# VectorE order around the gates: convolution channel 7 placed ahead of them, and the second layer's second S5 half placed behind the convolution

## The reference, cut to what matters

```python
for l in range(DEPTH):
    h = x @ w_in[l]
    s5_u, mq, mk, mv, gq, gk, gv, gz, ga, gb = _split(h, IN_SIZES)
    y_s5 = s5_mixer(s5_u, ...)          # states = associative_scan(a1*a2, a2*s1+s2)
    y_moba = moba_mixer(mq, mk, mv)
    y_gdn = gdn_mixer(gq, gk, gv, gz, ga, gb, ...)
    x = layer_norm(DEEPNORM_ALPHA * x + concat([y_s5, y_moba, y_gdn]) @ w_out[l], ...)
    f = swiglu(x, ...) if l % 2 == 0 else moe_ffn(x, ...)
    x = layer_norm(DEEPNORM_ALPHA * x + f, ...)

def gdn_mixer(q, k, v, z, a, b, conv_w, a_log, dt_bias, norm_w):
    qkv = silu(causal_conv(concat([q, k, v]), conv_w))      # 4 taps for each of 3*384 channels
    qh, kh = l2norm(heads(q)) * HEAD_DIM ** -0.5, l2norm(heads(k))
    beta = sigmoid(b)
    g = -exp(a_log) * softplus(a + dt_bias)                 # the gates
    o = chunk_gated_delta(qh, kh, heads(v), g, beta)        # solves (I + L) U = rhs in chunks of 64
```

## Time and profile before

| | us |
|---|---|
| time of the kernel before, median of 3 runs | 1582.57 (1580.28 to 1582.84) |
| the profiled execution, its own time | 1582.77 |
| span of the trace in it | 1581.0 |
| PE busy / DVE busy / ACT busy / POOL busy | 1538.6 / 1258.3 / 957.8 / 100.2 |

### The profile page before, as it was taken

How to read it: one execution, slowest core, us unless ns; L and a number is a source line. 1 busy time by engine, 2 the same in 40 slices (tenths; PEclk the granted TensorE clock), 3 DMA queues, 4 the chain that set the end, 5 groups by cost and what they waited for, 6 DMA issues and landing times.

```text
span 1581.0 us, 24154 instructions
## 1 busy us (share of the span) xinstructions
PE 1538.6 (97%) x9412; PEld 1268.5 (80%) x9412; DVE 1258.3 (80%) x1224; ACT 957.8 (61%) x811; POOL 100.2 (6%) x134
## 2 busy tenths in 40 slices
PE   8998999999998899999999999999999999999996
PEld 6777688888897767888888888888888888888875
DVE  6856854444788786888888888888888888888897
ACT  1175144334436524777777777777777777777774
POOL 0012180000000401000000000000000000000201
PEclk9999999999999999999999999999999999999999
DMA  9412488885354035999999999999999999999994
GB/s 335 161 55 82 160 318 307 279 280 186 107 175 173 9 131 200 395 393 394 395 396 361 395 396 350 395 396 349 395 396 351 395 396 349 395 396 368 398 394 162
DMA packets 195769, 473.12 MB, mean 299 GB/s; under 512 B 7712, under 2 KB 22176, under 8 KB 194640
## 3 DMA queue, kind: packets, MB, share of 16 engines
q1 hardware_dynamic: 191552, 454.23, 77.5%
q0 software_dynamic: 4144, 17.88, 2.9%
HBM read 464.21 MB, written 25.69 MB: 310 GB/s over the span
## 4 chain that ended last, share of the span: by engine, by line
PE 88%; DVE 7%; DMA 2%; issue 1%; ACT 1%; SPq 0%; DVEq 0%; ACTq 0%; POOLq 0%
PE ps L1865 47%; PE ps L1876 23%; PE ps L1815 4%; PE ps L1938 2%; PE ps L1843 1%; PE ps L2337 1%; PE ps L2333 1%; DVE arena L1197 1%; PE ps L1827 1%; DMA arena<-in_md 1%; DVE unit_lo L1295 1%; DMA arena<-in_w_in 1%; PE ps L2096 1%; PE ps L2233 0%; PE ps L2143 0%
## 5 line engine op out<-in xcount | busy, mean ns | idle before, releaser
L1289 DVE TENSOR_TENSOR lo<-arena,hi 128x2048 fp32r<-128x2048 f32 x378 | 865.2, 2292 | 206.0 <-ACT hi L732 205.6
L732 ACT ACTIVATE hi<-arena 128x2048 fp32r<-128x2048 f32 x378 | 724.4, 1919 | 353.9 <-PE ps L1865 230.3
L1865 PE MATMUL ps<-hi,xg 128*128 128x512 f32 x1760 | 542.7, 390 | 0.0
L1865 PEld LDWEIGHTS ps<-hi,xg 128*128 128x128 f32 x1760 | 329.7, 188 | 68.1 <-DVE lo L1289 0.2
L1865 PE MATMUL ps<-lo,xg 128*128 128x512 f32 x880 | 342.4, 389 | 0.0
L1876 PE MATMUL ps<-hi,hTe 128*128 128x512 f32 x896 | 282.5, 396 | 0.0
L1865 PEld LDWEIGHTS ps<-lo,xg 128*128 128x128 f32 x880 | 165.2, 188 | 34.3
L1876 PEld LDWEIGHTS ps<-hi,hTe 128*128 128x128 f32 x896 | 164.1, 188 | 32.0
L1876 PE MATMUL ps<-lo,hTe 128*128 128x512 f32 x448 | 175.1, 391 | 0.0
L1865 PE MATMUL ps<-hi,xs 128*128 128x512 f32 x512 | 159.4, 393 | 2.1 <-DVE xs L1622 1.1
L1865 PEld LDWEIGHTS ps<-hi,xs 128*128 128x128 f32 x512 | 96.1, 189 | 22.2 <-issue 2.5
(11 more groups left out here) (417 smaller groups left out, 1558.9 us busy)
## 6 DMA issues: line engine op xcount, KB each, us to landing
arena<-in_mg SPq DMA_DIRECT2D x112, 1024.0 KB, 7.7
arena<-in_mu SPq DMA_DIRECT2D x112, 1024.0 KB, 8.3
arena<-in_md SPq DMA_DIRECT2D x112, 1024.0 KB, 7.8
arena<-in_wg SPq DMA_DIRECT2D x14, 1024.0 KB, 5.2
arena<-in_wu SPq DMA_DIRECT2D x14, 1024.0 KB, 5.4
arena<-in_wd SPq DMA_DIRECT2D x14, 1024.0 KB, 5.2
arena<-in_w_in SPq DMA_DIRECT2D x10, 1024.0 KB, 5.7
xg_rows<-in_zeros SPq DMA_DIRECT2D x17, 512.0 KB, 7.5
```

Source lines behind the costliest of these rows:

```text
L732: af(hi[r % PARTS][:, :], raw[r % RAWS], ACT.Copy).then_inc(hi_ready, 1)
L1289: tt(lo[r % PARTS][:, :], raw[r % RAWS], hi[r % PARTS][:, :].bitcast(F32), ALU.subtract)\
L1865: ins = mm(ps[:, (4 if w == "G" else 4 + nb) + b, :], tok[a][:, kk * nt + b * P:kk * nt + (b + 1) * P], tiles_of(part[r % PARTS], w)[:, k, ...
```

## The change

Only the order of the DVE stream changes; nothing is computed otherwise and no other engine's code is touched. The same 987 DVE rows stand in another order. In the first layer the taps of channels 6 and 7 stand ahead of `gates_in`. In the second layer the six channels 0 to 5 and the split of the last weight unit stand ahead of the second S5 half, and channel 7 stands right ahead of `gates_in`; channel 6 stays behind it. The taps of channel 7 are gone from the inverse in both layers, and those of channel 8 stay.

```diff
@@ second layer, ahead of the gates
                     unit_low(9)
-                    s5_recur(l, 1)
-                    s5_turn(l, 1)
+                    convolve(l, 0)
                     score_sums_turned()
-                    convolve(l, 0)
                     convolve(l, 2)
                     convolve(l, 4)
                     unit_low(10)
+                    s5_recur(l, 1)
+                    s5_turn(l, 1)
@@ both layers
+                if l:
+                    convolve(l, 7, 1)
+                else:
+                    convolve(l, 6)
                 gates_in(l)
...
                 step.then(v_.reciprocal(beta, beta))
-                convolve(l, 6, 1)
+                if l:
+                    convolve(l, 6, 1)
@@ in the inverse
-                        if v < 2:
-                            for w in (((), (), (0, 1, 2, 3)), ((0, 1), (2,), (3,)))[v][g]:
-                                tap(l, 7 + v, w)
+                        if v == 1:
+                            for w in ((0, 1), (2,), (3,))[g]:
+                                tap(l, 8, w)
```

## The result

| | before | after |
|---|---|---|
| median of the runs side by side, us | 1582.26 (1580.28 to 1582.84, 4 runs) | 1570.89 (1567.47 to 1571.64, 4 runs) |
| ratio, 95% interval | | 0.9926 (0.9913 to 0.9938) |
| a second set: median, us | 1581.56 (11 runs) | 1571.32 (1570.76 to 1573.01, 5 runs) |
| ratio of that set | | 0.9942 (0.9929 to 0.9955) |
| span of the profiled execution | 1581.0 | 1569.2 |

The kernel became faster by 11.4 us in the first set and by 10.2 in the second; 1573.1 (1570.4 to 1577.0) was predicted. The lines of the code behind `gates_in` have moved: by 4 or 5 in DVE's code, by 5 in PE's (L2224 is L2229 now, L2124 is L2129, L1518 is L1523, L1444 is L1448, L1452 is L1457).

A forecast was written before the change was run, and what follows sets the result against it. The prediction took PE to be the bound, idling where it waits for DVE's or ACT's work in the mixers. Its terms, 4.0 + 2.4 + 0 + 3.3 = 9.7 us, off 1582.8 gave 1573.1 us, range 1570.4 to 1577.0.

The forecast's parts named there:

- Term 1: First layer's inverse: without channel 7's taps PE's 2.44 us gap closes and the clock no longer falls; 4.0 us gain.
- Term 2: Second layer's inverse: the same 2.44 us gap closes, clock full before and after; 2.4 us gain.
- Term 3: First layer's gates: channels 6 and 7 fit DVE's idle 10.30 us, and DVE was not late there; 0 us.
- Term 4: Second layer ahead of its gates: earlier squares close PE's 4.57 us gap, key products come earlier; 3.3 us gain.
- the price of the new idle time: Second layer, behind PE's new gap ahead of the decay: 0 if the clock stays, 1.0 or 2.7 us if it falls.
- the cover: Inverse, second pass: slack before PE needs group 1's subtraction; 1.4 us, or 0.8 if channel 8's first tap is held too.
- A: Both inverses: channel 8's held taps make group 1 late, giving back up to 1.7 us per layer; 1576.5, chance 0.08.
- B: Second layer: convolution or unit split held 3 us by ACT's exponentials, so gates, decay and key products slide; 1576.1, chance 0.07.
- C: Only the clock-free part arrives, or a late weight load catches the mixers' end; about 1580 to 1582, chance 0.04.
- D: Experts: an earlier start meets a weight stream without slack and PE waits; slower, 1586, chance 0.03.

The follow-up runs named there:

- experiment 2: Kernel before (as `e2_s5`), only the second layer's second S5 half moved behind the convolution, channel 7 left in the inverse; 1575.30 against 1581.75 us, ratio 0.9965.
- experiment 5: Kernel before, with POOL's third product of each inverse waiting until DVE has done group 0 of the second pass; 1579.13 against 1581.97 us, ratio 0.9981.
- experiment 4: Kernel before, with channel 7's fourth tap moved ahead of channel 8's last tap in the inverse's second pass; 1583.49 against 1581.75 us, ratio 1.0013.
- experiments 2 and 6: 6: changed kernel, second layer's channel 7 taps moved from ahead of the gates into DVE's idle inverse time; 1570.78 against 1581.56 us, again 1569.67 against 1581.97.
- e3_layer0: Kernel before, with channels 6 and 7 ahead of the gates in the first layer only, second layer as before; 1577.19 against 1581.75 us, ratio 0.9975.

## Why the prediction was right, point by point

**Term 1** (4.0): the mechanism as told, 3.83 measured. DVE was the last by 0.19 us, and not PE itself as predicted: `product_a(2, 0)` waited that long for DVE's L1525, since DVE's two subtractions began at 121.23, not at the 121.07 that the prediction had on this kernel's clock (122.56 less 1.49). Of the 4.0, the 1.6 of the clock were booked as certain. They are not: the gap of experiment 2 in the same place left the clock at full. The sure part is the gap: 2.24 us here (125.89 less 122.16, less the 1.49 of head start), and 2.31 between the 12.99 of experiment 2 and 10.68.

**Term 2** (2.4): 2.38.

**Term 3** (0): 0.07, from `gates_in` to the first subtraction.

**Term 4** (3.3): 4.21 to the key products, 4.07 with the 0.14 given back behind them. The working held in each of its steps: squares 5.2 us earlier, gap closed, new idle time of 2.58 for some 2.4 predicted, key products bounded by the scaled q and k. What was mis-sized is the price of the new idle time, 1.0: the clock did not fall behind it in either profile of the changed kernel, so nothing was paid, the lower of the two cases named.

**The sum.** 9.7 was predicted; the stretches give 10.4, of which the difference is this price (+1.0) and small terms (-0.3). The remaining 1.4 us by which the profiled span was better than the sum are the head of the program, which the prediction had held equal in both executions. The medians, 11.4 and 10.2 us, stand on either side of the sum so found.

That the time lies in the stated range is in part luck. The bounds of the terms ended at 1572.1 and the forecast with the chance of 0.70 was 1572 to 1575; the measured 1570.89 is below both, in the tail down to 1570.5 that had a chance of 0.08 for another reason, a clock fall that goes away by chance. The stretches without the head give 1582.77 - 10.4 = 1572.4, inside the forecast; what took the profiled execution of the changed kernel below it is the head.

**What became late next.** The hold on channel 8 came, with the cover as foreseen. The prediction had the second tap held; it was the first, for 1.44 us, so that group 1 (L1523 at 124.02, 0.88 us for the pair) ended at 124.9, which is 126.4 on the clock of the kernel before. That is the time that the rule of the Trainium skill gave (SBUF — State Buffer, "Who interferes with whom": a `tensor_scalar` in one of its fast modes contends with POOL too); on this the trace agrees with it, against the 125.8 of the sum. POOL's hold, inferred ahead from one duration, is shown by experiment 5.

**Rivals.** A (the hold moves and is paid) did not decide here but did in experiment 4, by 0.2 us of overlap with an instruction that had not been costed. B (the S5 half costs what it gains) had the right engine and the wrong step: the S5 half delayed nothing, but channel 7 ahead of the second layer's gates costs 1.95 us there (experiments 2 and 6). The prediction counted its 1.9 us into DVE's 503.0, saw that the gates do not get earlier through DVE, and did not ask what they would do without channel 7. The two halves of the change alone gave 6.4 and 6.5 us, 12.8 in sum against the 11.4 or 10.2 of both. C and D did not come: the stretch from the second inverse to the end is 1044.55 and 1044.50.

**What stays open.** Behind or at the end of PE's idle times of 2.44 us in the inverse the clock fell in three of seven cases (before, both times in the first layer only; `e2_s5` in the second only; `e3_layer0`, second layer, not). Behind the 4.57 us it fell in all six, behind the 3.06 us of experiment 4 in both, behind the 2.58 us ahead of the decay in none of two, behind the 0.89 and 0.92 us of the inverse never. So the length of the idle time alone does not decide at 2.44 us; what does was not settled. Nor was why the half clock among the first experts is longer in some executions.

## What to carry to other kernels

A step that is moved out of one bound place should be costed at its new place by asking what that place would do without it: channel 7 gained 2.4 us where it left and cost 1.95 where it arrived, and it is free in the idle times of 0.5 to 1.0 us that the receiving engine has while it waits. When two engines exclude each other, move the instructions by their times and look at every instruction behind them, the tiny ones too. And a gain from the clock behind a gap of some 2.5 us is a chance, not a term; the gap itself is the term.

## What the runs showed of the hardware that was not expected

- POOL's product (1.8 us) held a DVE `tensor_scalar` of 128x256 for 1.44 instead of 0.35 us, a `scalar_tensor_tensor` for 1.95 to 2.04 instead of 0.48, and a product of 128x12 for 1.78 instead of 0.16. The subtractions with one operand in PSUM kept 0.42 us beside it.
- After an idle time of the same 2.44 us the granted clock was 0.50 in three cases and 1.00 in four; a fall cost 1.3 to 1.5 us in the inverse (14.26, 14.51 against 12.99; 14.21 against 12.83).
- The landing of the first weights and the first 96 matmuls behind it took different times in two executions (by 0.67 and 0.82 us), and over twelve profiles the first layer's gates began at 97.14 to 98.99. The way from the second inverse to the end took 1043.71 to 1044.55 where the half-clock stretch of the first experts was short and 1045.83 and 1046.10 where it was about twice as long. Each is as much as a small edit is worth, and to be taken out of a comparison of two profiles first.
